# Two transformer blocks on one core: the first block's up projection on 512 positions, with the convolution's one earlier position computed apart by VectorE and ScalarE

## The reference, cut to what matters

```python
h2 = rmsnorm(h_res, g_ffn_pre[l])
up = centred_dwconv(h2 @ w_up[l], conv_w_ffn[l], conv_b_ffn[l])   # taps at -1, 0, +1
a, v = jnp.split(up, 2, axis=-1)
ffn_out = (jax.nn.gelu(a) * v) @ w_down[l]
h_res = h_res + rmsnorm(ffn_out, g_ffn_post[l])
return h_res[:, N_META:]
```

## Time and profile before

| | |
|---|---|
| time, median of 3 runs | 1572.82 us (1572.55 to 1572.91) |
| profiled execution | 1572.51 us, of which the span is 1570.7 |
| TensorE busy / clock granted | 1562.4 us, 99% / 0.999 of full speed |
| VectorE busy | 1104.7 us, 70% |
| ScalarE busy | 567.8 us, 36% |
| HBM traffic | 148.73 MB read, 98 GB/s over the span |

### The profile page before, as it was taken

How to read it: one execution, slowest core, us unless ns; L and a number is a source line. 1 busy time by engine, 2 the same in 40 slices (tenths; PEclk the granted TensorE clock), 3 DMA queues, 4 the chain that set the end, 5 groups by cost and what they waited for, 6 DMA issues and landing times.

```text
span 1570.7 us, 24508 instructions
## 1 busy us (share of the span) xinstructions
PE 1562.4 (99%) x9450; PEld 1410.6 (90%) x9450; DVE 1104.7 (70%) x1591; ACT 567.8 (36%) x820; POOL 41.1 (3%) x112
## 2 busy tenths in 40 slices
PE   9999999999999999999999999999999999999998
PEld 9999999999999988998889898888889888888886
DVE  7334466799888842288899998965657999888224
ACT  5123333542222232263333444477335422232122
POOL 4100000000000000000001011000000000000000
PEclk9999999999999999999999999999999999999999
DMA  6532223233322233233333233223331333323333
GB/s 200 140 100 87 87 68 94 68 108 95 93 93 83 91 107 105 84 108 94 106 102 88 81 88 92 90 81 94 96 101 60 121 95 93 96 92 93 107 94 94
DMA packets 47066, 151.94 MB, mean 97 GB/s; under 512 B 5835, under 2 KB 9959, under 8 KB 46992
## 3 DMA queue, kind: packets, MB, share of 16 engines
q1 hardware_dynamic: 44688, 146.21, 30.2%
q0 software_dynamic: 2160, 4.68, 1.3%
q10 hardware_dynamic: 144, 0.00, 0.0%
HBM read 148.73 MB, written 4.51 MB: 98 GB/s over the span
## 4 chain that ended last, share of the span: by engine, by line
PE 97%; DVE 2%; DMA 0%; ACT 0%; issue 0%; SPq 0%; DVEq 0%
PE ps L580 74%; PE ps L803 8%; PE ps L590 6%; PE ps L963 4%; PE ps L622 1%; PE ps L1014 1%; PE ps L914 1%; PE ps L693 0%; DVE tmp L1563 0%; PE ps L993 0%; PE ps L1002 0%; DVE res L1576 0%; PE ps L983 0%; DVE wlo L1492 0%; DVE xl L1532 0%; DMA res<-x_dram 0%
## 5 line engine op out<-in xcount | busy, mean ns | idle before, releaser
L580 PE MATMUL ps<-xh,whi 128*128 128x258 f32 (+2 forms) x1800 | 492.7, 324 | 0.1
L580 PE MATMUL ps<-xh,wlo 128*128 128x258 f32 (+2 forms) x1800 | 490.3, 323 | 0.0
L580 PE MATMUL ps<-xl,whi 128*128 128x258 f32 (+2 forms) x1800 | 489.5, 322 | 0.0
L1066 ACT ACTIVATE whi<-raw 128x1024 fp32r<-128x1024 f32 x268 | 283.3, 1057 | 487.2 <-DMA raw<-w_dram 466.3
L1492 DVE TENSOR_TENSOR wlo<-raw,whi 128x1024 fp32r<-128x1024 f32 x268 | 326.5, 1219 | 166.9 <-ACT whi L1066 166.2
L580 PEld LDWEIGHTS ps<-xh,whi 128*128 128x128 f32 x1800 | 301.6, 189 | 27.6 <-issue 0.7
L580 PEld LDWEIGHTS ps<-xl,whi 128*128 128x128 f32 x1800 | 301.4, 189 | 26.3 <-issue 0.5
L580 PEld LDWEIGHTS ps<-xh,wlo 128*128 128x128 f32 x1800 | 300.7, 189 | 26.7
L1897 DVE SCALAR_TENSOR_TENSOR work<-cin,vecs,work 128x512 f32<-128x512 f32 x240 | 180.2, 751 | 6.9
L1618 DVE TENSOR_TENSOR stage<-ps,rstd 128x516 f32<-128x516 f32 x57 | 39.6, 695 | 65.1 <-PE ps L580 63.1
L1625 DVE SCALAR_TENSOR_TENSOR work<-stage,vecs,work 128x512 f32<-128x512 f32 x88 | 66.1, 752 | 9.3 <-DVE work L1622 1.2
(11 more groups left out here) (265 smaller groups left out, 2326.1 us busy)
## 6 DMA issues: line engine op xcount, KB each, us to landing
raw<-w_dram SPq DMA_DIRECT2D x268, 512.0 KB, 3.5
bias_copies_dram<-bias_rows_dram POOLq DMA_DIRECT2D x12, 192.0 KB, 4.0
res<-x_dram SPq DMA_DIRECT2D x8, 264.0 KB, 5.6
out_dram<-res SPq DMA_DIRECT2D x8, 256.0 KB, 2.4
raw<-w_dram SPq DMA_DIRECT2D x4, 256.0 KB, 4.8
dftp<-dftp_dram POOLq DMA_DIRECT2D x1, 550.7 KB, 4.5
bias<-bias_copies_dram POOLq DMA_DIRECT2D x4, 128.0 KB, 2.6
bias<-bias_copies_dram POOLq DMA_DIRECT2D x8, 64.0 KB, 2.7
```

Of the source, the lines that this page charges most:

```text
L580: last = pe.matmul(ps[:, bank, 0:b - a], w[:, slot, cols], xx[:, k, a:b], start=start and n == 0, stop=stop and n == 2)
L1066: act.activation(whi[:, slot, :], raw[:, slot, :], ACT.Copy).then_inc(w_hi, 1)
```

## The change

The up stage of the first block works on positions 16 to 527 only, 512 columns in one bank a tile, and so uses the bank tables of the second block. Position 15, which the first tap of position 16 needs, is computed apart. VectorE forms the column of the residual at that position times the gain (`column`, 128x8), GpSimd stores it and loads it back as a row of 1024 on every partition (into `tmp`). GpSimd then loads, for each of the 44 tiles, the 128 channels' weights a second time with channels on the partitions (`lone_w`, 128x1024, 512 KB, two buffers). VectorE multiplies the two in place, ScalarE sums along the row (`accum_out` into `dots`), and VectorE multiplies the sum by `rstd` into `stage` one position ahead of the tile. ScalarE also takes over the first tap and the rounding to `fh` (`gated_high`), and VectorE makes `fl` in the next pair (`gated_low`). ScalarE no longer takes tiles 0 to 2 out of PSUM. The post-norm halves of the product before (`out1`) are 260 and 256 positions instead of 258 and 258.

```diff
-PAIRS_OF = {"u": (0, 3, 1, 0), "up1": (3, 0, 1, 3, 0, 1, 2, 3, 0, 1, 2, 3),
+PAIRS_OF = {"u": (0, 3, 1, 0), "up1": (0, 1, 2, 3, 6, 7, 5, 4, 0, 1, 2, 3),
-BY_ACT = {"u": 3, "up1": 3, "glu": 0, "up2": 0}
+BY_ACT = {"u": 3, "up1": 0, "glu": 0, "up2": 0}
+LONE = N_META - 1 - CUT
...
+            pool.wait_ge(column_ready, 1)
+            pool.dma_start(column_dram[0, :].rearrange("(p k) -> p k", k=KD), column[:, :]).then_inc(column_stored, 16)
+            pool.wait_ge(column_stored, 16)
+            pool.dma_start(tmp[:, :, :].rearrange("p a n -> p (a n)")[:, 0:D],
+                           bass.AP(column_dram.tensor, 0, [[0, P], [1, D]])).then_inc(column_spread, 16)
+            for n in range(2 * KFF):
+                if n >= 2:
+                    pool.wait_ge(lone_summed, n - 1)
+                pool.dma_start(lone_w[:, n % 2, :], lone_in[n]).then_inc(lone_landed[n % 2], 16)
...
+            up_row1 = [(N_META, L1)]
+            up_half1 = [(N_META, N_META + SEQ // 2), (N_META + SEQ // 2, L1)]
...
-            out_tiles("out1", "post1", (mgh, mgl), row1, row1, READY["merged"] - KD)
-            ffn("up1", "down1", (xh, xl), cut1, cut1, "h1f", "f1", "post1", "pre1f", "post1f")
+            out_tiles("out1", "post1", (mgh, mgl), row1, half1, READY["merged"] - KD)
+            ffn("up1", "down1", (xh, xl), up_row1, up_half1, "h1f", "f1", "post1", "pre1f", "post1f")
...
+                def lone_sum(it, s):
+
+                    act.wait_ge(lone_multiplied, it * 4 + (s + 1))
+                    act.activation(lone_w[:, s % 2, :], lone_w[:, s % 2, :], ACT.Identity,
+                                   accum_out=dots[:, s:s + 1]).then_inc(lone_summed, 1)
+
+                def first_tap(it, s):
+
+                    act.wait_ge(tile_read, it * 4 + (T0[up] + s + 1))
+                    if s % 2:
+                        if not isinstance(it, int) or it or s // 2:
+                            act.wait_ge(gated, it * 2 + s // 2)
+                    elif not isinstance(it, int) or it or s:
+                        act.wait_ge(gelu_ready, it * 2 + s // 2)
+                    m = it * 2 + s // 2
+                    act.activation(work[:, 2 * (s % 2), 0:SEQ], stage[:, s % 2, 2:2 + SEQ], ACT.Identity,
+                                   scale=vec("conv_w_ffn", m + (s % 2 * KFF + 2 * KFF)),
+                                   bias=vec("conv_b_ffn", m + s % 2 * KFF)).then_inc(tap_ready, 1)
+
+                def gated_high(m):
+
+                    act.wait_ge(gated, m + 1)
+                    f_hi = fh[:, m, :] if isinstance(m, int) else fh[:, ds(m, 1), :].rearrange("p a n -> p (a n)")
+                    act.activation(f_hi, work[:, 3, 0:SEQ], ACT.Copy).then_inc(gated_hi, 1)
+
                 def up_body(it, ahead=False):
                     for s in range(4):
+                        if up == "up1" and s % 2 == 0 and (not isinstance(it, int) or it or s):
+                            gated_high(it * 2 + (s // 2 - 1))
                         if not ahead:
                             w_to_hi(up, it, s + 3)
                         elif s % 2:
                             for n in HI_AHEAD.get(it * 2 + s // 2, ()):
                                 w_to_hi(up, 0, n)
+                        if up == "up1":
+                            lone_sum(it, s)
+                            first_tap(it, s)
...
+                def gated_low(m):
...
+                    dve.wait_ge(gated_hi, m + 1)
+                    dve.tensor_tensor(f_lo, work[:, 3, 0:SEQ], f_hi.bitcast(F32), ALU.subtract).then_inc(operand_ready, 1)
...
+                            if up == "up1":
+                                dve.wait_ge(lone_landed[s], it * 32 + 16 * (h + 1))
+                                dve.tensor_tensor(lone_w[:, s, :], lone_w[:, s, :], column_row, ALU.mult) \
+                                   .then_inc(lone_multiplied, 1)
+                            bank = PAIRS_OF[up][it_n + n] if it_n + n < len(PAIRS_OF[up]) else n
+                            scaled(up, it * 4 + n, bank, stage[:, s, 2:2 + SEQ], N1 - SEQ if up == "up1" else 0)
+                            if up == "up1" and s == 0 and (not isinstance(it, int) or it or h):
+                                gated_low(it * 2 + (h - 1))
...
+                            if up == "up1":
+                                dve.wait_ge(lone_summed, it * 4 + (n + 1))
+                                step(dve.tensor_tensor(stage[:, s, 1:2], dots[:, n:n + 1], rstd[:, LONE:LONE + 1], ALU.mult))
+                                dve.wait_ge(tap_ready, it * 4 + (n + 1))
+                            else:
+                                step(dve.tensor_scalar(row, stage[:, s, off + 1:off + 1 + SEQ],
...
+            dve.wait_ge(res_ready, UPDATE_AT["post1"] + 2 * KD)
+            gains = vecs[:, VCOL["g_ffn_pre"]:VCOL["g_ffn_pre"] + KD]
+            dve.tensor_tensor(column[:, :], res[:, :, N_META - 1:N_META].rearrange("p k a -> p (k a)"), gains, ALU.mult) \
+               .then_inc(column_ready, 1)
+            step(dve.memset(stage[:, :, 2 + SEQ:4 + SEQ], 0.0))
             inverse_of_res("up1", "pre1f", N1)
+            dve.wait_ge(column_spread, 16)
```

More of the change, by code:

```diff
@@ L254, in two_block_kernel @@
         lowest = put("lowest", [P, 8])
+        column = put("column", [P, KD])
+        dots = put("dots", [P, 4])
         shares = put("shares", [P, 2, 8])
@@ L387, in two_block_kernel @@
         gelu_ready = sem("gelu_ready")
+        column_ready = sem("column_ready")
+        column_stored = sem("column_stored")
+        column_spread = sem("column_spread")
+        lone_landed = [sem(f"lone_landed{s}") for s in range(2)]
+        lone_multiplied = sem("lone_multiplied")
+        lone_summed = sem("lone_summed")
+        tap_ready = sem("tap_ready")
+        gated = sem("gated")
+        gated_hi = sem("gated_hi")
         taps_done = sem("taps_done")
@@ L679, in three @@
                 def three(p, k, h):
[L680 to L681 removed]
+                    return half_passes(pairs[p], h * SEQ // 2, p, k, k, operand, spans[h], k == 0, k == KD - 1)
                 pe.wait_ge(w_split, C0[phase] + 1)
@@ L688, in high @@
                 def high(p, ks):
-                    bank, at_ = (2 * pairs[p], 0) if phase == "up1" else (pairs[p], 0)
                     a, b = spans[0]
@@ L1086, in unscaled @@
                 piece_used(phase, n)
-                dst = ut[:, n, :] if phase == "u" else stage[:, n, 0:width] if n < 2 else tmp[:, n - 2, 0:width]
                 pair = PAIRS_OF[phase][n]
-                act.activation(halves(dst), ps[:, 2 * pair:2 * pair + 2, 0:width // 2], ACT.Identity) \
+                act.activation(halves(ut[:, n, :]), ps[:, 2 * pair:2 * pair + 2, 0:width // 2], ACT.Identity) \
                    .then_inc(tile_read, 1)
@@ L1097, in squares_of_res @@
                     act.activation(sq[:, k % 2, 0:b - a], res[:, k, a:b], ACT.Square).then_inc(sqp_ready, 1)
-                    if k == 1 and phase == "up1":
-                        unscaled(phase, 0, b - a)
                 if phase != "u":
                     w_to_hi(phase, 0, 4)
-                for n in range(1 if phase == "up1" else 0, BY_ACT[phase]):
+                for n in range(BY_ACT[phase]):
                     unscaled(phase, n, b - a)
@@ L1689, in two_pairs @@
                         after_step()
-                        step(dve.tensor_tensor(work[:, 3, 0:SEQ], work[:, 1, 0:SEQ], work[:, 2, 0:SEQ], ALU.mult))
+                        last = dve.tensor_tensor(work[:, 3, 0:SEQ], work[:, 1, 0:SEQ], work[:, 2, 0:SEQ], ALU.mult)
+                        if up == "up1":
+                            last.then_inc(gated, 1)
+                            continue
+                        step(last)
                         after_step()
@@ L1702, in ffn @@
                     two_pairs(it)
-                loop(KFF // 2, 14, two_pairs, first)
+                loop(KFF // 2, 14 if up == "up2" else 10, two_pairs, first)
+                if up == "up1":
+                    gated_low(KFF - 1)
                 if dn == "down2":
```

128 lines of the change are left out of this document (66 added, 62 removed).

## The result

The changed kernel takes 1581.27 us (median of 4 runs, 1581.01 to 1581.82) beside 1572.68 for the kernel before: ratio 1.0057, interval 1.0044 to 1.0069. It is **8.6 us slower**, where 3.6 were forecast. The profiled execution has a span of 1579.1.

What follows compares the result with a forecast made beforehand. TensorE was taken to set the up stage's pace, with VectorE close behind. TensorE's 13.5 us gain against 17.1 lost through VectorE's late chain made 3.6 us slower than 1572.82: 1576.4 us, range 1569.5 to 1583.

Steps and rivals of the forecast that it cites:

- likeliest case: First up stage: VectorE's late chain delays the down product; 1576.4 us, alone 1573.8 to 1580.3, chance 0.55.
- first slot starts: VectorE's first scaling in the up stage, held by the first weight load: 13.0 us after its last `xl`.
- slots 2, 4, 10, 14: Unrolled tiles whose split waits 1.65 us for a high part behind ScalarE's sum and tap: 6.79 us each.
- even / odd slots with a split: VectorE's steps in an unrolled tile that also splits a weight: 5.14 us even, 5.32 odd.
- slot 16 starts: End of the 16 unrolled tiles on VectorE, start plus all slots: 102.0 us after its last `xl`.
- loop pair: Two loop tiles on VectorE, 5.34 and 5.46 us: 10.80 against TensorE's 10.89, fourteen times.
- f complete: Last gated product's high and low parts ready for the down product's third piece: 254.6 us after the last `xl`.
- third rival: VectorE's new product does not overlap neighbours, 1580.4 us, or its loop waits cost 0.1 more each, 1582; chance 0.17.
- rule beside the sum: VectorE: its first half has operations wait for an empty pipe, about 17 us more; its second lets unheld ones start earlier.
- TensorE alone: First up stage with 512-column matmuls at 0.2268 us, if nothing keeps TensorE waiting: 13.5 us gained.
- TensorE idle in no loop tile, VectorE without a wait for TensorE: Expected signs in the new profile's up stage, VectorE's from tile 0 to the stage's end.
- last rival: `lone_w` loads take over 8.4 us from issue to landing; at 9.0, 13 us more, 1590 us; chance 0.09.

Runs made afterwards that it cites:

- e4: The change with GpSimd issuing the first two `lone_w` loads ahead of the column's store and broadcast; 1581.74 us.
- e1: The change with ScalarE making high parts 7, 9, 14 and 17 ahead of the even tile's sum and tap; 1574.13 us.
- e2: The change with position 15's loads, product and sum left out (sum set to zero); 1563.49 us.
- e5: e1 with scaling ahead of the product, tap ahead of the sum, and the tap needing position 15 last; 1568.69 us.
- e7: e2 with the first up stage's operand in aligned rows of 2048 bytes; 1558.78 us.
- e11: The change with the first up stage's operand in aligned rows of 2048 bytes, nothing else; 1582.84 us.
- e10: e7 with the operand's rows of 2048 bytes all starting 64 bytes behind a multiple of 512; 1562.69 us.
- e9: e7 with the operand in rows of 2112 bytes again, each read from its first byte; 1563.34 us.
- e6: e5 with the first up stage's operand in aligned rows of 2048 bytes; 1565.17 us.
- e8: e6 with weights 10 to 17 split earlier in the first up stage; 1563.67 us.
- e12: e8 with splits 6 to 16 another slot earlier, and VectorE waiting for the column only before its first product; 1563.34 us.
- e3: The change with the 128x1024 product moved from VectorE to GpSimd; 1647.64 us.

## Why the prediction was right, and where its sizes were off

The direction, the place and the mechanism held: VectorE's chain is late, and the down product's third piece waits for f. The time lies 4.9 us above the forecast, inside the range (1569.5 to 1583) and 1 us outside the likeliest case's own. Against the zero (VectorE's last `xl`, now 314.26), the third piece starts at 259.8, forecast 254.7, before 251.2; the difference of 8.6 to before is the whole measured loss. The 5.1 beyond the forecast are 0.8 at the start, 1.5 in the written-out slots, 2.6 in the loop and 0.2 at the end, from these terms of its sum:

| term | forecast | measured |
|---|---|---|
| first slot starts | 13.0 | 13.8 |
| slots 2, 4, 10, 14 | 6.79 each | 6.94 |
| even / odd slots with a split | 5.14 / 5.32 | 5.18 / 5.40 |
| slot 16 starts | 102.0 | 104.3 |
| loop pair, 14 of them | 10.80 | 10.98 |
| f complete | 254.6 | 259.6 |

- *The start.* The load was late as worked out, but by more than was taken: 13.8 is near the upper of the bounds, 12.15 to 14. The first load took 6.95 us from issue to landing beside the broadcast and the weight stream, and landed 13.7 behind the zero, past the 13.2 that the forecast had for two loads one after the other. e4 shows that turning the order round doesn't mend it.
- *The late high parts.* Four waits of 1.67 against 1.65. e1 removed them and got 7.1 us, 6.6 by the forecast. The other written-out slots came out 0.04 to 0.10 long each; in those with a split it is the one-column product, 0.26 to 0.28 to the next tap where 0.20 was taken.
- *The new product overlaps its neighbours*, 1.14 against 1.13, so that part of the third rival is out, and with it what the first half of the rule beside the sum would have made of it (the Trainium skill, VectorE: DVE Perf Modes, "The DRAIN you can't avoid"); the trace agrees with the second half. That leaving out position 15's work turns the sign was shown by e2.
- *The loop.* This is the term that was most off, half of the 5.1. The even tile took the 5.34 of the forecast, the odd one 5.64 instead of 5.46. I gave the loop's waits 0.1 each and did not see that in the odd tile ScalarE's tap, behind the sum, comes later than VectorE wants it: the tap is 0.08 longer than its row, and in the loop VectorE starts 0.23 behind its end, where 0.03 was seen in tile 0. That makes 0.32 of waiting in every odd tile. The third rival's other half (VectorE's own waits cost more) did not come true, though its 1582 is near what was measured: that nearness is chance. e5 shows that this was order, not work.
- *TensorE alone* was taken as 13.5 us, at the second block's 0.2268 a matmul. It is 9.3 in this layout (e2) and 14.0 in an aligned one (e7). The sum took TensorE to be ready at 253.0; it was at 258.4 (tile 17 starts at 411.68; 27 tiles of 5.56 and 48 matmuls of 0.2268 behind it is 572.7), by its slower matmuls and the half clock, although it had waited only 11.7 us by tile 17 (15.3 forecast). In the loop it was the slower engine, 11.12 a pair against VectorE's 10.98, so VectorE made good 1.9 us of its lag, and still ended 1.1 later. So this error, of 5.4 us, cost nothing in the time (e11). That was luck: it stayed hidden because VectorE's chain was late by about as much. Where VectorE's chain is shorter, as in e5, TensorE is the bound.
- *TensorE idle in no loop tile, VectorE without a wait for TensorE*: both as told. TensorE's first waits came before tiles 6, 7 and 9, the longest (4.76) before tile 10, since slot 5 has no split.
- *The loads late* (last rival): only the first. The up stage moved 166 to 206 GB/s, and GpSimd's loads landed in 3.9 us (median).

## What to carry to other kernels

- Ask of an added instruction not only its length, but what stands behind it on its own engine's queue and what another engine wants from there. Of the 8.6 us lost, 7.1 came back when four high parts were moved ahead of two instructions. Another 5.4, which makes it faster than the kernel before, came when scaling and tap changed places with product and sum. No work was taken away.
- When two engines are within 2% of each other, read both chains. A fault on the one that waits (the rows of the operand here) is invisible until the other is mended, and then it is the next thing to pay for.
- A matmul's price is that of its operand's layout too: take it from a stage whose rows lie in the same way.

## What the runs showed of the hardware

- A matmul of 512 fp32 columns steps 0.2267 us when the rows of its moving operand are 2048 bytes apart and the first starts on a multiple of 512, 0.2290 with all starts shifted by 64 bytes, 0.2317 with rows 2112 bytes apart: up to 2.2% (e7, e10, e2 and e9). With rows 2112 bytes apart the steps repeat with every fourth row, as the starts do against 256 bytes.
- The granted clock fell to 1.2 GHz, and matmuls to 0.43 us apart, around the end of waits of TensorE of 1.9 to 4.9 us (this change, e1, e4, e5, e6, e8, e11, e12): at the earliest 2.3 us before the end of the wait, and so inside it, at the latest 1.4 us behind it. It stayed there for 6.8 us with the waits of 4.2 us and more, and for 3.4 with the shorter ones. Two waits of 1.9 in the change had no such sequel. In e2, e7, e9 and e10, where TensorE does not wait in the stage, the clock stayed up.
- VectorE began 0.23 us behind the end of the ScalarE tap that it waited for in the loop, and 0.03 behind it in the written-out tile 0.
- GpSimd's product of 128x1024 took 2.4 us, and two VectorE instructions with two inputs in SBUF that met one took 2.2 and 2.4 us longer than alone (e3).
- Two loads of 512 KB ahead of a 4 KB store on GpSimd's queue made GpSimd wait 6.9 us for the store instead of 3.3 (e4).
